# Weighted one-hot rows in a PEER routing stage: two VectorE masks and four ScalarE scalings, or one VectorE mask and four fused VectorE rows

## The reference

```
v1, i1 = top_k(s1, 16); v2, i2 = top_k(s2, 16)        # per token and head, 128 keys on each side
top_s, pos = top_k(v1[..., :, None] + v2[..., None, :], 16)
idx = take_along_axis(i1 * 128 + i2, pos);  wgt = softmax(top_s)
act = gelu(einsum('bphkd,bpd->bphk', u_tab[idx], x))
out = einsum('bphk,bphkd->bpd', wgt * act, v_tab[idx])
```

## Time and profile before

| | |
|---|---|
| device time, median of 3 runs | 4703.05 us (4690.11 to 4716.12) |
| profiled execution, first to last instruction (span) | 4686.6 us |
| mean granted PE clock | 0.982 |
| PE busy | 4418.1 us, 94% |
| DVE busy | 3104.3 us, 66% |
| POOL busy | 2694.0 us, 57% |
| ACT busy | 1796.3 us, 38% |
| L2346, DVE masks, 384 of 128x512 | 244.2 us busy, 676 ns each |
| L1664, ACT scalings, 768 of 128x128 | 243.9 us busy, 399 ns each |
| L1209, PE one-hot products | 214.8 us busy, 101.9 us idle ahead of them, ended by ACT |

### The profile page before, as it was taken

The page is one execution under the profiler, slowest core; times in us unless marked ns, Lnnn a source line. Parts: engine busy times, 40 slices in busy tenths (PEclk is TensorE's granted clock), DMA queues, the critical chain, the costliest instruction groups (busy, mean ns, idle before and its releaser), DMA issues.

```text
span 4686.6 us, 73672 instructions
## 1 busy us (share of the span) xinstructions
PE 4418.1 (94%) x21322; PEld 3672.7 (78%) x21322; DVE 3104.3 (66%) x5261; ACT 1796.3 (38%) x3291; POOL 2694.0 (57%) x1477
## 2 busy tenths in 40 slices
PE   7999999999989989999989999999999899999998
PEld 6766775789988987887767667757898888978777
DVE  5654224438889877888866551244488897778888
ACT  3134114123566653333341441231245656633333
POOL 5842663565456665555558337636654566755554
PEclk9998999999999999999999999999999999999999
DMA  2210221224689999999822112212246889999997
GB/s 102 90 50 32 81 81 48 69 78 134 180 262 281 305 311 311 345 340 339 304 89 90 47 38 87 77 41 77 80 140 183 266 272 316 330 319 345 341 340 269
DMA packets 455706, 877.23 MB, mean 187 GB/s; under 512 B 45248, under 2 KB 314048, under 8 KB 452672
## 3 DMA queue, kind: packets, MB, share of 16 engines
q1 hardware_dynamic: 376064, 602.54, 39.8%
q0 software_dynamic: 73728, 268.47, 16.5%
q10 hardware_dynamic: 5696, 3.85, 0.3%
HBM read 779.27 MB, written 95.42 MB: 187 GB/s over the span
## 4 chain that ended last, share of the span: by engine, by line
PE 65%; DVE 10%; issue 10%; DMA 8%; POOL 3%; ACT 3%; SPq 1%; DVEq 0%; ACTq 0%; POOLq 0%
PE pair L833 6%; PE bank L833 6%; PE bank L1235 5%; DMA ring<-v_tab 5%; PE bank L1178 5%; PE bank L1240 5%; PE bank L1230 4%; PE bank L859 3%; PE pair L859 3%; PE pair L835 3%; PE bank L835 3%; PE bank L1182 2%; PE bank L995 2%; PE bank L900 2%; DMA ring<-u_tab 2%
## 5 line engine op out<-in xcount | busy, mean ns | idle before, releaser
L687 POOL TENSOR_TENSOR w_hi<-ring,ones 128x1024 fp32r<-128x1024 f32 x272 | 537.1, 1975 | 810.1 <-PE bank L859 279.3
L675 POOL TENSOR_TENSOR w_lo<-ring,w_hi 128x1024 fp32r<-128x1024 f32 x256 | 615.4, 2405 | 509.7 <-ACT w_hi L1632 508.7
L1178 PE MATMUL bank<-xT,w_hi 128*128 128x384 f32 x2048 | 719.9, 352 | 19.1 <-ACT qk L1648 7.7
L690 POOL TENSOR_TENSOR w_lo<-ring,w_hi 128x1024 fp32r<-128x1024 f32 x272 | 693.4, 2549 | 21.4
L1178 PE MATMUL bank<-xl_peer,w_hi 128*128 128x384 f32 x2048 | 698.6, 341 | 0.0
L1638 ACT CAST w_hi<-ring 128x1024 fp32r<-128x1024 f32 x252 | 265.5, 1054 | 649.6 <-PE bank L1240 427.1
L1632 ACT CAST w_hi<-ring 128x1024 fp32r<-128x1024 f32 x256 | 269.0, 1051 | 570.7 <-DVE ring L2314 467.6
L2411 DVE TENSOR_TENSOR cl<-att,ch 128x384 fp32r<-128x384 f32 x256 | 350.7, 1370 | 148.4 <-ACT ch L1707 135.3
L681 POOL TENSOR_TENSOR w_lo<-ring,w_hi 128x1024 fp32r<-128x1024 f32 x126 | 301.9, 2396 | 250.9 <-ACT w_hi L1638 250.9
L1178 PEld LDWEIGHTS bank<-xT,w_hi 128*128 128x128 f32 x2048 | 396.3, 194 | 22.8 <-ACT w_hi L1632 14.2
L1235 PE MATMUL bank<-w_hi,cl 128*128 128x512 f32 x1524 | 391.3, 392 | 16.3 <-DVE cl L2411 16.3
(11 more groups left out here) (364 smaller groups left out, 9273.6 us busy)
## 6 DMA issues: line engine op xcount, KB each, us to landing
ring<-v_tab SPq DMA_DIRECT2D x252, 512.0 KB, 6.2
ring<-w_stream SPq DMA_DIRECT2D x240, 512.0 KB, 3.2
ring<-u_tab SPq DMA_DIRECT2D x512, 128.0 KB
g_spill<-gst SPq DMA_DIRECT2D x240, 192.0 KB, 4.2
vg<-w_spill SPq DMA_DIRECT2D x64, 704.0 KB, 10.7
hn<-u_tab SPq DMA_DIRECT2D x256, 128.0 KB
x_last<-u_tab SPq DMA_DIRECT2D x256, 128.0 KB
w_spill<-vg SPq DMA_DIRECT2D x12, 2048.0 KB, 9.1
```

The costliest lines, as they stand in the source:

```text
L675: nc.gpsimd.tensor_tensor(w_lo[s % 2][:, :], ring[2 + s % 2][:, :], w_hi[s % 2][:, :].bitcast(F32), ALU.subtract)\
L687: nc.gpsimd.tensor_tensor(w_hi[b][:, 0:n], src, ones[:, 0:1].to_broadcast([P, n]), ALU.mult)\
L690: nc.gpsimd.tensor_tensor(w_lo[b][:, 0:n], src, w_hi[b][:, 0:n].bitcast(F32), ALU.subtract)\
L1178: nc.tensor.matmul(out, w_hi[s % 2][:, c * P:(c + 1) * P], dense_parts(c)[part], start=(c == 0 and part == 0), stop=False)
```

## The change

DVE makes the weighted rows by itself. The column of e1 for all 128 tokens of a tile is copied once from PSUM to `pick1` in SBUF (the weights were copied there before), and DVE waits for that copy. Then in each slot one `tensor_tensor` makes the mask `hot2` of four tokens as before, and four `scalar_tensor_tensor`, one for each token, make the rows of `hot1`: (column number equals e1) times w, with e1 as a per-partition scalar from SBUF and w as a PSUM column that is broadcast. The last one raises `hot_ready`. ACT's `scale_hot` and the semaphore `ones_ready` are gone.

```diff
-        pickw = floor[:, 0, 0:P]
+        pick1 = floor[:, 0, 0:P]
...
-        ones_ready = Count(sem("ones_ready"), dict(UW=(WROUNDS, 4)))
...
+        pick_step = Count(sem("pick_step"), dict(P=(DENSE, 1)))
...
-                def scale_hot(k, s):
-
-                    b, at = s % 2, 16 * (k % 8) + 4 * s
-                    act.wait_ge(ones_ready.sem, ones_ready.at(L, "UW", k, s + 1))
-                    for j in range(4):
-                        ins = nc.scalar.activation(hot1[b][:, j, :], hot1[b][:, j, :], ACT.Copy,
-                                                   scale=pickw[:, at + j:at + j + 1])
-                    ins.then_inc(hot_ready.sem, 1)
-
                 def round_of(i, last=False, k=None, tile=DENSE):
 
                     for s in range(4):
-                        if k is not None:
-                            scale_hot(k, s)
...
                     if k % 8 == 0 and s == 0:
-                        V.tensor_copy(pickw, pickT[:, 2, :])
-                    for z in range(2):
-                        ins = V.tensor_tensor(hot[b][:, z, :, :], pickT[:, z, at:at + 4].unsqueeze(2).to_broadcast([P, 4, N_KEYS]),
-                                              iota_k[:, :].unsqueeze(1).to_broadcast([P, 4, N_KEYS]), ALU.is_equal)
-                    ins.then_inc(ones_ready.sem, 1)
+                        c = Chain(dve, pick_step, L, "P", k // 8)
+                        c.step(V.tensor_copy(pick1, pickT[:, 0, :]))
+                        c.wait()
+                        c.close()
+                    V.tensor_tensor(hot2[b], pickT[:, 1, at:at + 4].unsqueeze(2).to_broadcast([P, 4, N_KEYS]),
+                                    iota_k[:, :].unsqueeze(1).to_broadcast([P, 4, N_KEYS]), ALU.is_equal)
+                    for t in range(at, at + 4):
+                        ins = V.scalar_tensor_tensor(out=hot1[b][:, t - at, :], in0=iota_k[:, :], scalar=pick1[:, t:t + 1],
+                                                     in1=pickT[:, 2, t:t + 1].to_broadcast([P, N_KEYS]),
+                                                     op0=ALU.is_equal, op1=ALU.mult)
+                    ins.then_inc(hot_ready.sem, 1)
```

## The result

| | before | after |
|---|---|---|
| median, 7 runs of each on one chip | 4705.81 us (4690.11 to 4716.12) | 4730.21 us (4721.19 to 4734.57) |
| ratio to before, 95% interval | | 1.0047 [1.0031, 1.0063] |
| profiled execution, span | 4686.6 us | 4724.3 us |
| mean granted PE clock | 0.982 | 0.976 |
| DVE, ACT, PE busy | 3104.3, 1796.3, 4418.1 us | 3188.7, 1592.9, 4439.0 us |

The kernel is 0.47% slower, some 22 to 24 us. The forecast was 7 us faster, and the result lies 2 us outside the range.

A forecast was written before the change was run, and what follows sets the result against it. DVE's work was taken to bound the heavy stretch (slots 24 to 87), while the light one (88 to 119) had DVE room. Heavy +9 and light -16 gave -7 us, 4703 to 4696 us, range 4662 to 4728.

The forecast's parts named there:

- the prices on the engines: New rows at a pitch of 0.26 us; DVE busy rises to about 3190 us, ACT falls to about 1555.
- the 29.4 of the prediction: DVE work added in each layer's heavy stretch, slots 24 to 87: 64 x 0.46 = 29.4 us.
- no lock: DVE's new rows beside POOL: the SBUF pointer doesn't count as a second SBUF input, so no stretching expected.
- how short the way becomes: From a late turn's start to PE's expert products: 3.0 us without the scaling, against 6.65 before.
- -16 us in the light stretches: Slots 88 to 119, both layers: somewhat over half of PE's 28.7 us of waits for rows is gained.
- the pattern of a late turn: After a late load, PE's expert products start 6.65 us after turn; the change saves PE up to 3.6 us.
- +9 us in the heavy stretches: Slots 24 to 87, both layers: 4.4 and 2.2 us more, plus 1 to 2 a layer for waits that don't vanish.
- three waits: DVE's heavy-stretch waits that can vanish: for PE 14.4 us, the tile's transposes 5.4, data 5.2 in the first layer.
- small gaps: DVE idle time between dependent steps in the first heavy stretch: 11.3 us expected to stay.
- DVE's idle time stays: Rival, heavy stretch: added work paid in full, +43 us, 4746 us, if under two fifths of waits is absorbed; chance 0.13.
- both sums: Forecast: +9 - 16 = -7 us; rival with DVE's idle time staying: 2 x 29.4 - 16 = +43 us.
- the forecast's own signs of being wrong: Pitch under 0.22 or over 0.3 us, heavy-stretch PE idle well under 35 us, or light stretches that don't shorten.

The follow-up runs named there:

- e6: Against e2, two of every four u_tab loads fetch only half of their 512 KB, so the output isn't the reference's: 4623.51 us, ratio 0.9832.
- e4: Against the changed kernel, 18 dot row products of the sparse tile moved from slots 38 to 87 into slots 88 to 127: 4734.12 us, ratio 1.0066.
- e7: Against e2, 10 dot row products moved from slots 88 to 127 into slots 38 to 87: 4670.58 us, ratio 0.9938.
- e1: Against the kernel before, the masks are not scaled at all, so the expert weights are left out: 4685.64 us, ratio 0.9959.
- e2: Against the kernel before, ACT scales slot n+1's masks ahead of the rounding of slot n+2: 4686.68 us, ratio 0.9958.
- e3: Against the changed kernel, ACT also copies the finished rows onto themselves, times one, at the old queue place: 4733.38 us, ratio 1.0068.
- e9: Against the changed kernel, each 2 MB store is cut in four and spread among the loads: 4712.22 us, ratio 1.0007.
- e8: Against the changed kernel, DVE makes the four weighted rows of a slot twice, once into a scratch buffer: 4854.84 us in one run.

## Why the prediction was wrong

**Right: the prices on the engines.** A row follows the last one 0.255 to 0.258 us behind its start (0.26 predicted). DVE is busy 3188.7 us (3190). DVE's 28.7 us more in the first heavy window are the 29.4 of the prediction. The rule that the prediction cites from the Trainium skill ("VectorE: DVE Perf Modes", "The DRAIN you can't avoid") would make the pitch the row's full 0.34 us; the runs show 0.26, and DVE's busy time would otherwise be some 60 us higher. The prediction left out how that section goes on: a next operation that is not held starts earlier. With this the trace agrees. ACT is busy 1592.9 us, where about 1555 was predicted. The windows show (225.39 - 158.50) / 64 = 1.05 us less for a slot; I had taken the 1.26 us that one group spans in the timeline for what it adds to the busy time.

**Right: no lock.** 768 rows with an SBUF tensor and an SBUF pointer beside POOL at 57% took 347 ns at most. By the rule of the Trainium skill in "SBUF — State Buffer" ("SBUF: two separate sides") the 355 of them that lie beside one of POOL's subtractions could have stretched if the pointer counted as a second SBUF input. None did.

**Right: where the wait goes, and how short the way becomes.** PE's wait left the one-hot products for the first expert product, and a late turn reaches PE in 2.85 us (3.0 predicted). But I read this as a gain by itself. In the first heavy stretch PE still waits 34.6 us, as often as before, since DVE is the one that is late, and PE's waits are only how this shows at PE.

**Wrong: -16 us in the light stretches.** It was about 0 (-4.1 and +2.9). The step that failed is "in the light stretch this is a true gain, for DVE has room". I compared with PE and DVE and never with the transfers, though the numbers stood in the earlier trace rows: a DMA share of 1.02 and 1.04 at 315 and 326 GB/s, against 0.84 and 0.83 at 252 and 250 in the heavy stretches. The light stretch goes by its transfers. e6 shows it alone (-5 MB, -22 us, with the work of every engine as it was); e4 (+8 MB, +21 us with 52 us of DVE idle time) and e7 (-6 MB, -14 us) agree from both sides; e1, e2 and e3 move the queue and DVE's work and leave the late slots at 222 to 230 us. That length times GB/s comes to 58.7 and 58.6 MB before and 58.5 and 58.6 after shows nothing of this: the same work moves the same bytes whatever bounds it, and the heavy stretches agree as well (92.6, 92.5, 92.4 and 92.3 MB). The 9.2 us wait that I took for the pattern of a late turn is a load that was issued behind a 2 MB store. What PE saves after such a wait is probably waited for at later loads: DVE's turn waited 51.2 us for `ring`'s loads over the kernel before and 58.1 after, but no run follows a single load through.

**Wrong: +9 us in the heavy stretches.** It was +28.8 (+23.6 when cut at PE). The term that was mis-sized is DVE's idle time that remains: 11.3 us, with 1 to 2 added, against 22.1 measured (381.9 - 359.8). I let three waits vanish, 25 us. One did, the 14.4 us for PE to be through with the mask buffer. The wait for the tile's transposes went from 5.4 to 3.8 us and that for data from 5.2 to 5.3 (in the second layer from 6.5 to 7.6). Another 1.7 us stand against an event that the profile could not name, and some 11 to 12 are the small gaps, as forecast. The waits for data hang on the big stores: DVE's list of waits has none of them in e9, where the stores are split. It has none in e8 either, with 60 us more work, and 1.0 to 2.3 us in e3 and e4, so they can shrink, but in the change itself they stayed. In e8 16 us of idle time are left even so.

**The rivals.** "DVE's idle time stays" named the place and the direction, and at 4746 us it is nearer to 4730 than the forecast is. Its condition, less than two fifths of the idle time absorbed, was not met: 14.2 of 25 us were. Slower it was all the same, since the -16 that both sums took along wasn't there. Of the forecast's own signs of being wrong, one came: the light stretches didn't shorten. With -16 set to nothing the forecast's sum gives 4703 + 9 = 4712 us, and with only the heavy term corrected 4703 + 28.8 - 16 = 4716; either miss alone would have left it within 0.5%. Both together give 4732. That this comes within 2 us of 4730 is partly luck, as single profiles scatter by more.

**Open.** The spans differ by 10 us more than these stretches explain, and the medians don't call for it; the part from slot 127 to the next layer's slot 0 alone scatters by 17 us. PE's busy time in the first heavy window is 8.9 us higher after, at a clock of 0.97 instead of 0.99. It lies beside DVE's work, and whether the stretch would be shorter at the higher clock was not tried.

## What to carry to other kernels

Before a wait is priced as a gain, read the window's DMA share and GB/s beside the engines: here a share of 1.02 to 1.06, with room on every engine, marked the stretches where a freed queue bought nothing. The test is a run with fewer bytes and the same work. Where one engine is 90% busy, don't count all of its idle time as room for more work: here its waits for a buffer vanished, those for late transfers stayed at first and the small gaps stayed, and added work was paid from half to nine tenths. When an instruction is late because of its place in a queue, try the place first: moving the scalings gave 0.42%, moving their work to the engine that bounds the stretch cost 0.47%.

## What the runs showed of the hardware

- Loads are issued more slowly behind a large store in the same queue. Four loads of 128 KB take 1.9 us to issue, and behind a 2 MB store mostly 4.2 to 4.9 us, once 6.2. With the stores cut in four and spread (and SP's loop written out), the same 73 MB move at 333 to 337 GB/s instead of 322, and the kernel gains 0.6% (0.9958 to 0.9898).
- A DVE instruction with a pointer scalar took a little longer than one without. Of the same operation over 1024 columns, the one with a constant scalar (`dot`, L2353) holds DVE 1.14 us, from 1442.24 to 1443.38, and the one with a pointer (`add_row`) 1.19. The mask of 512 columns holds it 0.57 us and line L1776, with the pointer, 0.66. Rows of 128 columns follow each other at 0.26 us and MAX8 at 0.19. The pairs differ in more than the pointer, so its share isn't isolated.
- DVE instructions without a wait between them overlap: the rows last 0.34 us each and start 0.26 us apart.
- The granted PE clock fell behind a lump of idle time. Windows of after around the wait of 3.32 us that ends at 1446.23 (columns as above):

```profile
1441.00:1446.20 5.20, 1.91 (x14) 1.72 (x13) 5.11 (x11) 1.46 (x3) 0.33 (x1) 1.00 0.41 128
1446.20:1449.50 3.30, 3.27 (x14) 3.27 (x15) 3.06 (x8) 0.97 (x1) 3.02 (x2) 0.71 0.50 171
1449.50:1453.00 3.50, 3.50 (x21) 3.50 (x20) 3.50 (x14) 2.44 (x3) 2.54 (x2) 0.78 0.90 267
1453.00:1457.00 4.00, 4.00 (x26) 4.00 (x25) 3.85 (x8) 1.00 (x2) 1.74 (x2) 1.00 1.01 412
```

PE is idle for 3.3 us. The granted clock is 1.00 until then, 0.71 and 0.78 in the next two windows (so part of each at 1.2 GHz and the rest at 2.4), and 1.00 again from 1453. The expert products start 0.17 to 0.18 us apart up to 1447.6 and 0.32 us apart from 1447.9 to 1450.4.
